# Two blocks on one Trainium2 core: the norm and first transposes behind the experts by column halves, and the last expert's tail inside both arms of a branch

## What is computed

```
# layer l of the first block, l = 0, 1
h = layer_norm(ALPHA * h + mix, ln_mix_g[l], ln_mix_b[l])
h = layer_norm(ALPHA * h + moe(h, ...), ln_ffn_g[l], ln_ffn_b[l])     # "behind the experts"
# what reads h next: l = 0: proj = h @ [nsa_w_kv | nsa_w_in]; l = 1: proj = rms_norm(h, pre_mix_g) @ w_in
y = (x - mean) / sqrt(var + eps) * g + b                               # layer_norm, over the 1024 columns
y = y + w[:, e:e+1] * ((silu(x @ w_gate[e]) * (x @ w_up[e])) @ w_down[e])   # each of 16 experts
```

## Time and profile before

| | us |
|---|---|
| median of 3 runs (1366.15 to 1367.99) | 1367.03 |
| the profiled execution | 1372.42 |
| its span in the trace | 1370.6 |
| PE busy | 1299.0 (95%) |
| DVE busy | 710.1 (52%) |
| ACT busy | 551.1 (40%) |

### The profile page before, as it was taken

One profiled execution on the slowest core, in us unless ns is written; L12 is line 12 of the kernel. 1 busy time (PEld: TensorE's weight loads), 2 busy tenths in 40 slices (PEclk: granted clock), 3 DMA queues, 4 the chain that ended last, 5 costly groups with the idle time before them and its releaser, 6 DMA issues.

```text
span 1370.6 us, 16899 instructions
## 1 busy us (share of the span) xinstructions
PE 1299.0 (95%) x6808; PEld 909.6 (66%) x6808; DVE 710.1 (52%) x1123; ACT 551.1 (40%) x819; POOL 74.5 (5%) x78
## 2 busy tenths in 40 slices
PE   7999998999999699998999999599999999799998
PEld 5887886444443487676444443278888877799986
DVE  4766656222211585886222221466674566678772
ACT  4445443121212343682211111345556653465561
POOL 0000000000000000000000000005770000000000
PEclk9999998999999899998999999799999999899999
DMA  9653558999999765308799999854455335455540
GB/s 340 201 182 123 175 194 337 383 420 421 422 421 421 256 208 167 122 1 337 317 422 422 420 422 421 308 181 155 153 156 172 133 124 166 155 184 179 184 162 31
DMA packets 103890, 342.52 MB, mean 250 GB/s; under 512 B 10188, under 2 KB 17020, under 8 KB 79100
## 3 DMA queue, kind: packets, MB, share of 16 engines
q1 hardware_dynamic: 97056, 331.57, 64.1%
q10 hardware_dynamic: 6748, 9.77, 2.1%
HBM read 340.27 MB, written 1.05 MB: 249 GB/s over the span
## 4 chain that ended last, share of the span: by engine, by line
PE 86%; DVE 7%; ACT 3%; issue 2%; DMA 1%; ACTq 1%; DVEq 0%
PE PS L679 23%; PE PS L1341 16%; PE PS L526 9%; PE PS L1375 9%; PE PS L604 7%; PE PS L582 5%; PE PS L1323 3%; PE PS L1351 1%; PE PS L1385 1%; PE PS L2010 1%; DVE wlo L491 1%; PE PS L663 1%; PE PS L731 1%; PE PS L1737 1%; PE PS L1763 1%
## 5 line engine op out<-in xcount | busy, mean ns | idle before, releaser
L491 DVE TENSOR_TENSOR wlo<-raw,whi 128x2048 fp32r<-128x2048 f32 (+1 forms) x122 | 273.9, 2264 | 112.5 <-ACT whi L485 107.9
L485 ACT ACTIVATE whi<-raw 128x2048 fp32r<-128x2048 f32 (+1 forms) x122 | 224.8, 1875 | 32.1 <-PE PS L582 13.9
L1341 PE MATMUL PS<-moe_ring,xg 128*64 128x512 f32 x896 | 198.0, 592 | 0.0
L679 PE MATMUL PS<-whi,th 128*128 128x512 f32 x480 | 191.2, 398 | 2.7 <-ACT a_proj L2900 1.5
L679 PE MATMUL PS<-whi,tl 128*128 128x512 f32 x480 | 187.2, 390 | 0.0
L679 PE MATMUL PS<-wlo,th 128*128 128x512 f32 x480 | 187.0, 390 | 0.0
L1341 PEld LDWEIGHTS PS<-moe_ring,xg 128*64 128x64 f32 x896 | 64.9, 137 | 126.5 <-issue 124.7
L1492 DVE TENSOR_TENSOR hidden<-hidden,PS 64x512 f32<-64x512 f32 x32 | 22.1, 690 | 172.1 <-ACT hidden L1448 172.1
L1481 DVE SCALAR_TENSOR_TENSOR y_split<-PS,w_slot,y_split 64x512 fp32r<-64x512 f32 x64 | 48.0, 750 | 121.0 <-ACT y_split L1433 119.9
L679 PEld LDWEIGHTS PS<-whi,th 128*128 128x128 f32 x480 | 90.2, 188 | 23.3 <-DVE wlo L491 2.0
L1375 PE MATMUL PS<-moe_ring,hT 128*64 128x512 f32 x448 | 102.3, 598 | 1.1 <-ACT hT L1455 0.9
(11 more groups left out here) (397 smaller groups left out, 1967.7 us busy)
## 6 DMA issues: line engine op xcount, KB each, us to landing
moe_ring<-in_moe_w_gate SPq DMA_DIRECT2D x56, 1024.0 KB, 13.7
moe_ring<-in_moe_w_up SPq DMA_DIRECT2D x56, 1024.0 KB, 15.1
moe_ring<-in_moe_w_down SPq DMA_DIRECT2D x56, 1024.0 KB, 16.2
raw<-in_w_in SPq DMA_DIRECT2D x32, 1024.0 KB, 5.3
raw<-in_ret_w_in SPq DMA_DIRECT2D x24, 1024.0 KB, 5.2
raw<-in_w_up SPq DMA_DIRECT2D x20, 1024.0 KB, 5.2
raw<-in_w_down SPq DMA_DIRECT2D x10, 1024.0 KB, 5.0
raw<-in_ret_w_out SPq DMA_DIRECT2D x8, 1024.0 KB, 5.0
```

The lines of the kernel that those rows point to most:

```text
L485: nc.scalar.activation(s.whi[:, high, 0:kc, 0:wide], s.raw[:, slot, 0:kc, 0:wide], ACT.Copy).then_inc(s.hi_done, 1)
L491: nc.vector.tensor_tensor(s.wlo[:, slot, 0:kc, 0:wide], s.raw[:, slot, 0:kc, 0:wide], s.whi[:, high, 0:kc, 0:wide], ALU.subtract).then_inc ...
L679: last = nc.tensor.matmul(PS[:, 2 * (col % 2) + tt, 0:wide], x[:, KC * kb + c, tt * P:(tt + 1) * P], w[:, k, c, 0:wide], start=(kb == 0 an ...
L1341: m = nc.tensor.matmul(PS[64 * k:64 * k + 64, gate_up_bank(e), :], x, moe_place(layer, n)[:, c, :], start=(half == 0 and c == 0), stop=(ha ...
```

## The change

1. In layer_norm behind the experts, tile 0 is normed by column halves: DVE waits for each half's scatter, takes bn_stats half by half, and writes X by halves; each half counts `normed`, and PE transposes a half as soon as it is written.
2. Tile 1's mean and variance move from DVE to ACT: a Copy of the 1024 PSUM columns with a running sum, a scaling by -1/D, and a Square with that bias and a running sum, both written to token_sq. DVE's order becomes norm tile 0, tl half 0, split_lo b0, tl half 1, split_lo b0+1, norm tile 1 by halves, tl of both halves. ACT's becomes split_hi b0, the sums, roots and th of tile 0, split_hi b0+1, th of tile 1, and then all DMA issues; in layer 1 both Squares of X stand behind th of tile 1.
3. The opening waits for each half by itself (half_hi, then half_lo), takes th*whi, tl*whi, th*wlo one after the other, waits for hi_done and lo_done at their first use, and transposes tile 1 behind both blocks of tile 0. It is used for the first product of the program too.
4. The last y (ACT, DVE) and the last scatter (PE) stand in both arms of the branch, so the test and the jump come before them; ACT's Sqrt table is loaded before the last y.

The counts of `normed` and `squared` that others wait for are adapted (normed_count), and gained_turn_vector takes halves as half_turn_vector does. In layer 1 DVE's call is the same with gained_turn_vector. The core of the diff:

```diff
@@ -633,13 +635,10 @@
-            def opening(step):
-                if step == 0:
-                    pe.wait_ge(half_lo, 4 * k + 2)
-                if step == 1 and turn is not None:
+            def opening(tt, kb, low):
+                if tt == 1 and kb == 0 and not low and turn is not None:
                     turn()
-                if step == 2:
-                    pe.wait_ge(half_lo, 4 * k + 4)
+                pe.wait_ge(half_lo if low else half_hi, 4 * k + 2 * tt + kb + 1)
             return opening
...
@@ -651,15 +650,15 @@
                         b = l.b0 + kb
-                        if kb == 0:
-                            opening(2 * tt)
-                        elif tt == 0:
-                            opening(1)
-                        if tt == 0:
-                            pe.wait_ge(lo_done, b + 1)
-                        for c in range(KC):
-                            for i, (x, w, k) in enumerate(((xh, whi, b % HIGHS), (xh, wlo, b % RAWS),
-                                                           (xl, whi, b % HIGHS))):
+                        opening(tt, kb, False)
+                        for i, (x, w, k) in enumerate(((xh, whi, b % HIGHS), (xl, whi, b % HIGHS), (xh, wlo, b % RAWS))):
+                            if i == 1:
+                                opening(tt, kb, True)
+                            if tt == 0 and i == 0:
+                                pe.wait_ge(hi_done, b + 1)
+                            if tt == 0 and i == 2:
+                                pe.wait_ge(lo_done, b + 1)
+                            for c in range(KC):
                                 last = nc.tensor.matmul(
...
@@ -722,11 +721,14 @@
-        def half_turn_tensor(pe, k, source, ready, halves=range(TT)):
+        def half_turn_tensor(pe, k, source, ready, halves=range(TT), columns=None):
             for tt in halves:
-                ready(tt)
+                if columns is None:
+                    ready(tt)
                 for half in range(2):
+                    if columns is not None:
+                        columns(tt, half)
                     for c in range(4):
...
@@ -739,8 +741,8 @@
-        def half_turn_vector(dve, k, tt):
-            for half in range(2):
+        def half_turn_vector(dve, k, tt, halves=range(2)):
...
@@ -769,9 +771,17 @@
+        def normed_count(k, tt):
+            return k + tt + 1 + (2 if k > 2 else 0) + (2 if k > 6 else 0)
         def normed_by(pe, k):
-            return lambda tt: pe.wait_ge(normed, k + tt + 1)
+            return lambda tt: pe.wait_ge(normed, normed_count(k, tt))
+        def column_normed_by(pe, k):
+            return lambda tt, half: pe.wait_ge(normed, normed_count(k, 0) + 2 * tt + half)
...
@@ -1379,13 +1389,14 @@
                 pe.wait_ge(s.pickT_ready, v0 + e + 1)
-                pe.wait_ge(s.y_lo, 2 * (v0 + e + 1))
                 for tt in range(TT):
                     for half in range(2):
+                        if tt == 0:
+                            pe.wait_ge(s.y_lo, 2 * (v0 + e) + half + 1)
                         last = nc.tensor.matmul(PS[:, 2 * tt + half, :], pickT[:, e % 3, tt * P:(tt + 1) * P],
                                                 y_split[:, half, :], start=False, stop=False, skip_group_check=True)
-                    if e == E - 1 and tt == 0:
-                        last.then_inc(to_vector, 1)
+                        if e == E - 1 and tt == 0:
+                            last.then_inc(to_vector, 1)
                 last.then_inc(s.scattered, 1)
...
@@ -1417,8 +1428,7 @@
                 down(e)
-            scatter(E - 1)
-            return crowded
+            return crowded, lambda: scatter(E - 1)
...
@@ -1456,10 +1466,13 @@
                     turned_pick(e + 1, 7)
+                else:
+                    early_table(ACT.Sqrt)
                 if e == 8:
                     crowded = crowded_of(act, layer)
-                y(e)
-            return crowded
+                if e + 1 < E:
+                    y(e)
+            return crowded, lambda: y(E - 1)
...
@@ -2636,13 +2650,16 @@
             router_tensor(pe, st, k, layer)
-            crowded = paired_tensor(pe, paired, layer)
+            crowded, last_scatter = paired_tensor(pe, paired, layer)
             with pe.If(crowded > 0):
+                last_scatter()
...
+            with pe.Else():
+                last_scatter()
...
@@ -2653,16 +2670,31 @@
             params(act, st, norm_params(a["ln_ffn_g"][layer], a["ln_ffn_b"][layer]))
-            crowded = paired_scalar(act, paired, layer)
+            crowded, last_y = paired_scalar(act, paired, layer)
             with act.If(crowded > 0):
+                last_y()
...
-            for b in range(AHEAD):
-                split_hi(act, sweep_first, moe_b0[layer] + b, 0)
-            early_table(ACT.Sqrt)
+            with act.Else():
+                last_y()
+        def after_experts_scalar(act, o, layer, turned):
+            x = PS[:, 2:4, :].rearrange("p b n -> p (b n)")
+            b0 = moe_b0[layer]
+            split_hi(act, sweep_first, b0, 0)
+            act.wait_ge(paired.scattered, E * (layer + 1))
+            o.then(nc.scalar.activation(token_sq[:, :], x, ACT.Copy, accum_out=small[:, 72:73]))
+            o.then(nc.scalar.activation(small[:, 73:74], small[:, 72:73], ACT.Copy, scale=-1.0 / D))
+            root_half(act, 2 + 4 * layer, 0)
+            nc.scalar.activation(token_sq[:, :], x, ACT.Square, bias=small[:, 73:74],
+                                 accum_out=small[:, 74:75]).then_inc(squared, 1)
+            turned(0)
+            root_half(act, 2 + 4 * layer, 1)
+            split_hi(act, sweep_first, b0 + 1, 0)
+            turned(1)
...
@@ -2674,30 +2706,50 @@
             router_vector(dve, st, o, layer)
-            crowded = paired_vector(dve, paired, layer)
+            crowded, last_y = paired_vector(dve, paired, layer)
             with dve.If(crowded > 0):
+                last_y()
...
-        def experts_half(dve, st, o, tt, layer):
-            if tt == 0:
+            with dve.Else():
+                last_y()
+        def token_columns(tt, h):
+            return X[:, tt, h * BW:(h + 1) * BW]
+        def after_experts_vector(dve, st, o, layer, turned):
+            b0 = moe_b0[layer]
+            def norm_columns(tt, mean, first):
+                for h in range(2):
+                    cols = slice(h * BW, (h + 1) * BW)
+                    o(nc.vector.scalar_tensor_tensor(token_columns(tt, h), PS[:, 2 * tt + h, :], mean, gb[:, 0, cols],
+                                                     first, ALU.mult))
+                    if h == 0:
+                        inverse_half(dve, o, 2 + 4 * layer, tt)
+                    o.wait()
+                    nc.vector.scalar_tensor_tensor(token_columns(tt, h), token_columns(tt, h), small[:, 8 + tt:9 + tt],
+                                                   gb[:, 1, cols], ALU.mult, ALU.add).then_inc(normed, 1)
+            for h in range(2):
                 inbox(dve, st)
-            else:
-                dve.wait_ge(paired.scattered, E * (layer + 1))
-            for h in range(2):
-                o(nc.vector.bn_stats(small[:, 16 + 12 * tt + 6 * h:22 + 12 * tt + 6 * h], PS[:, 2 * tt + h, :]))
-            variance_half(o, tt)
-        def experts_norm_half(dve, o, k, tt):
-            o(nc.vector.scalar_tensor_tensor(X[:, tt, :], PS[:, 2 * tt:2 * tt + 2, :].rearrange("p b n -> p (b n)"),
-                                             small[:, 2 * tt:2 * tt + 1], gb[:, 0, :], ALU.subtract, ALU.mult))
-            inverse_half(dve, o, k, tt)
-            shift_half(tt)
+                o(nc.vector.bn_stats(small[:, 16 + 6 * h:22 + 6 * h], PS[:, h, :]))
+            variance_half(o, 0)
+            dve.wait_ge(params_in, 16 * st.params)
+            norm_columns(0, small[:, 0:1], ALU.subtract)
+            dve.wait_ge(squared, layer + 1)
+            nc.vector.tensor_scalar(small[:, 9:10], small[:, 74:75], 1.0 / D, LN_EPS, ALU.mult,
+                                    ALU.add).then_inc(norm_var, 1)
+            turned(0, (0,))
+            split_lo(dve, sweep_first, b0, 0)
+            turned(0, (1,))
+            split_lo(dve, sweep_first, b0 + 1, 0)
+            norm_columns(1, small[:, 73:74], ALU.add)
+            turned(1, (0, 1))
...
@@ -2741,13 +2793,14 @@
-            half_turn_tensor(pe, 2, tokens(X), normed_by(pe, 2), (0,))
-            nsa_in_tensor(pe, opened_by(pe, 2, lambda: half_turn_tensor(pe, 2, tokens(X), normed_by(pe, 2), (1,))))
+            half_turn_tensor(pe, 2, tokens(X), None, (0,), column_normed_by(pe, 2))
+            nsa_in_tensor(pe, opened_by(pe, 2, lambda: half_turn_tensor(pe, 2, tokens(X), None, (1,),
+                                                                        column_normed_by(pe, 2))))
...
-            half_turn_tensor(pe, 4, tokens(X), normed_by(pe, 6), (0,))
```

(35 more changed lines are left out.)

22 lines of the change are left out of this document (8 added, 14 removed).

## The result

The changed kernel took 1375.08 us (median of 4, 1374.32 to 1377.89) against 1366.86 for the kernel before (1366.15 to 1367.99): ratio 1.0056, interval [1.0043, 1.0069]. It is **slower by 8.2 us**; the forecast was +2.0 and no change. Its profiled execution took 1374.7, span 1372.9, and lies at its median, while that of the kernel before (1372.42) lay 5.6 above its own. So the two spans differ by 2.3 only, and the comparison has to be made stretch by stretch.

What follows compares the result with a forecast made beforehand. PE was taken as the bound (busy 95% of the span, 86% of the chain). Terms +0.1 + 2.4 - 2.85 + 2.4 gave +2.0, so 1369.0 us on the median, forecast as no change; eight-in-ten range 1361.0 to 1372.8.

Steps and rivals of the forecast that it cites:

- Part 1: Tail in the branch arms: scatter 0.45 later, DVE's 4.96 us stall in layer 1 gone, ACT's jump and table load hidden.
- rival (c): Jump at the end of PE's arm waits as the first does: +6.1, 1373.1; 12%.
- Parts 2 and 3: Behind the experts, the second column waits for b0+2: +0.1 in layer 0 (481.2), -2.85 in layer 1 (900.9).
- the opening's gain: PE's opening behind layer 0 gains 3.5, all idle time; in layer 1 5.2 of idle PE precedes the second column.
- rival (b): The opening's gain is kept because b0+2 is split earlier: up to -3.5 and -6.5, so 1357; 15%.
- Part 4: PE's clock falls after the new idles of 3.5 and 5.2 behind the experts, costing 2.4 each.
- Part 5: First product: opening ends 1.2 earlier, next block still waits for wlo of b0+2: 0; nothing, or one more clock loss.
- rival (d): Clock falls in the first product's opening too, or stays down 2.8 in each place: +2.8 to +4.4, 1371; 13%.

Runs made afterwards that it cites:

- Table_behind: The changed kernel with the early load of the root's table moved behind the join, between the split of b0 and the sum; 1373.5 us, ratio 1.0041.
- third_ahead: Table_behind with ACT's split of b0+2 moved ahead of its th of tile 1 and the DMA issues; 1359.4 us, ratio 0.9941.
- norm_first: Table_behind with DVE's norm of tile 1 ahead of the split of b0+1 and PE's turn between the blocks; 1365.7 us, ratio 0.9985.
- opening_only: The kernel before with only PE's new opening order (waits by quarters, wlo group last, tile 1 transposed behind both blocks); ratio 1.009, 12.9 us slower.
- opening_early_turn: opening_only with PE's transposes of tile 1 put back between the two blocks of tile 0; ratio 1.0012 to the kernel before.
- after_third: The changed kernel, table loads as they are, with ACT's split of b0+2 moved ahead of its th of tile 1; 1360.5 us, ratio 0.9957.
- tail_ahead: Table_behind with the last y and last scatter called ahead of the branch on PE, ACT and DVE; 1377.7 us, ratio 1.0066.
- no_pe_branch: third_ahead with PE's test and its arm (the sweep for crowded experts) taken out; ratio 0.9948 to the kernel before.

## Why the prediction was wrong

Between the forecast's +2.0 and the sum by rows at the end of this section, +8.2, lie 6.2 us: 2.6 and 2.25 because the two second columns start later than forecast, 1.6 in the first product, and -0.3 in the clock's terms. Point by point, by the prediction's own parts:

**Part 1, right in the main.** PE's test started at 449.12 (forecast 450.85, in a profile whose hT was 1.6 earlier), took 6.27, and the scatter began 6.95 behind hT against 6.53: +0.42 where 0.45 was forecast. DVE's stall in layer 1 went, y was in time, and no jump at an arm's end shows, so rival (c) fell. **What failed** is the sentence that ACT's table load comes "at 450.3 to 451.9, hidden". That load did nothing; two more of 1.28 stand behind the arms. I priced the instruction by its row and not by whether its effect outlives the branch.

The rows follow this step through my sum. I had ACT's sum start with the scatter's end, 8.2 behind hT; the first of the two loads pushed the split, which ended at 8.75 in both layers, and the sum started at 8.93 and 8.78. I had the root at 9.6; behind the second load it started at 11.59 and 11.44. I had X's first half ready at 10.75; PE transposed it at 12.91 and 12.75, 2 us late. Table_behind gives back 1.19 and 1.07 of these 2, since one load still stands ahead of its sum; no kernel without any was run.

**Parts 2 and 3, the size of the second column.** Behind hT I had 30.95 and 34.0; measured 33.58 and 36.30. Of these 2.6 and 2.3, 2 are there at the first transposes already, by the table loads; table_behind's second columns come 0.94 and 1.07 earlier. In layer 0 the four scatters took 1.94 instead of 1.16, since the clock fell at 455.67 already (459.1 in the earlier trace rows), but ACT was busy with the split until 0.14 before their end, so this cost 0.2 at most. The rest, 0.5 and 0.3, is small lateness in DVE's and ACT's steps, which the sum took back to back. That the second column waits for the split of b0+2 behind the DMA issues, and that the opening's gain is idle time, was right; third_ahead shows it by taking that away (rival (b)'s condition) and gaining 14 us.

**I saw the new order of DVE and underrated it.** My sum had X of tile 1 0.93 later than before (it came 3.1 later in layer 0 and 0.25 in layer 1) and moved on. Its price is all that hangs on it: norm_first, which puts the norm back first and turns tile 1 between the blocks, gained 7.8, half in time and half in clock. And the turn's place behind both blocks of tile 0, which stands in my sum without a price, costs 11 us where X is early (opening_only against opening_early_turn); in the changed kernel DVE's order hides it: PE is through both blocks and waits 0.79 for the second half of X (472.08). So the parts of this change don't add.

**Part 4, right** in that the clock fell in both places. I took 2.4 for each stretch; measured 1.7 and 2.9 in one profile, 1.7 and 1.4 in the other.

**Part 5, wrong.** "Nothing, or one more clock loss": it was the loss. Ten profiles show the new opening with the old split in the first product; in all PE idles 2.7 to 3.5 before the second column. In eight the clock fell behind it, and cost 1.6 to 2.8; in two (the changed kernel's first and table_behind's) it didn't. That was rival (d).

The sum by rows, changed kernel less kernel before (first profiles; the first product from the later ones): layer 0's second column +2.7, its clock +1.7; layer 1's -0.6 and +2.8; the first product +1.6 (the value most of those profiles show; its own two show 0 and 2.55). That is **+8.2**, the medians' difference; so close an agreement is luck, since the clock's terms vary by 1.4 to 2.5 from one execution to the next. The second profiles give +2.1, +1.5, -0.7, +1.4 and +2.55 for the same terms, +6.9. My +2.0 had +0.1, +2.4, -2.85, +2.4 and 0 for them.

Open: what sets whether and how long the clock is down after the same idle time (12.34 for the same 48 matmuls of layer 1's stretch in one profile of the changed kernel and 13.79 in the other), and whether DVE's stall goes by code addresses.

## What to carry to other kernels

When one engine's stretch is shortened, look at what the next block waits for and move that first; here one call, which puts the third block's split into ACT's idle time, turned a loss of 8 us into a gain of 7.5 (after_third). Idle time of PE ahead of dense work mostly cost twice here, as a wait and then as half clock, so a part that gains nothing by itself may still cost. And where instructions are moved around a branch, ask which state of the engine (a function table, fetched code) is still valid behind the join.

## What the runs showed of the hardware that was not expected

- A table loaded ahead of a branch was loaded again behind it: three loads of 1.28 us for one root, on ACT (449.01, 454.15, 458.91).
- Idle time of PE of 2.3 to 5.3 us ahead of dense matmuls was followed by 1.4 to 2.9 us of lost clock in 20 of 22 places (12 behind the experts, 10 in first products) and by none in two, with 2.8 and 3.3 of idle time. Idle time of up to 1.6 us cost at most 0.2.
- DVE's 4.96 us stall at a jump vanished when other code changed and its place in the work did not (tail_ahead).
- The jump of 6.2 us on PE cost nothing that the time shows where the down product and y covered most of it (no_pe_branch), and left PE idle for 5.28, 1.0 of it with X written, where it stood behind the scatter (tail_ahead).
